# PEER expert gathers: up and down row of a pick in one transfer, down rows multiplied on four 64x64 quarters of TensorE

## The reference, cut to what matters

```
s1, s2 = scores of the token's query against keys[0], keys[1]      # (128, 8, 128) each
v1, i1 = top_k(s1, 16); v2, i2 = top_k(s2, 16)
sv, pos = top_k(all 256 sums v1 + v2, 16);  eidx = i1 * 128 + i2 at pos
g   = softmax(sv)
act = gelu(einsum('thkd,td->thk', u_tab[eidx], xb))                 # up rows
out = einsum('thk,thkd->td', g * act, v_tab[eidx])                  # down rows
```

## Time and profile before

| | |
|---|---|
| median of 3 runs | 4980.2 us (4972.65 to 4982.28) |
| the profiled execution, its own time | 4965.21 us |
| span of the profiled execution, first to last instruction | 4963.3 us |
| mean granted TensorE clock | 0.850 of full speed |
| busy: PE, PEld, DVE, ACT, POOL | 3325.2, 1520.2, 2724.8, 734.2, 2441.9 us |
| moved by DMA | 1566.78 MB |
| first gather issued, last `add_up` starts | 923.6 us, 4943.9 us |

### The profile page before, as it was taken

The page is one execution under the profiler, slowest core; times in us unless marked ns, Lnnn a source line. Parts: engine busy times, 40 slices in busy tenths (PEclk is TensorE's granted clock), DMA queues, the critical chain, the costliest instruction groups (busy, mean ns, idle before and its releaser), DMA issues. The chain is left out here.

```text
span 4963.3 us, 57041 instructions
## 1 busy us (share of the span) xinstructions
PE 3325.2 (67%) x21891; PEld 1520.2 (31%) x21891; DVE 2724.8 (55%) x6844; ACT 734.2 (15%) x1873; POOL 2441.9 (49%) x2579
## 2 busy tenths in 40 slices
PE   8897888782655676745676666566667656555677
PEld 4443775540011331322232244134313411210111
DVE  1357443497665575555666565555566556556410
ACT  1045231110000031000021023103202200000000
POOL 0000000156666566556666655655566566566665
PEclk9995998896888888977887888788888888788899
DMA  5160001599999999999999998998999899999998
GB/s 206 54 271 22 6 5 44 185 355 362 371 372 384 393 371 368 398 379 381 385 388 368 379 389 331 367 390 318 346 384 399 323 358 406 362 371 374 371 367 324
DMA packets 426081, 1566.78 MB, mean 316 GB/s; under 512 B 50278, under 2 KB 51393, under 8 KB 419281
## 3 DMA queue, kind: packets, MB, share of 16 engines
q0 software_dynamic: 369088, 1342.53, 70.3%
q1 hardware_dynamic: 56424, 220.51, 11.6%
q10 hardware_dynamic: 298, 0.09, 0.0%
HBM read 1559.84 MB, written 3.10 MB: 315 GB/s over the span
## 5 line engine op out<-in xcount | busy, mean ns | idle before, releaser
L2212 PE MATMUL t_ps<-t_vring,t_wz 128*32 128x512 f32 x4864 | 1641.0, 721 | 868.7 <-DMA t_vring<-in_peer_v,t_eidT 467.0
L1691 DVE SCALAR_TENSOR_TENSOR t_uring<-t_uring,t_ps 128x1024 f32<-128x1024 f32 x1280 | 1555.6, 1217 | 1039.2 <-DMA t_uring<-in_peer_u,t_eidx 779.2
L1567 POOL DMA_INDIRECT t_vring<-in_peer_v,t_eidT x1216 | 1152.5, 948 | 921.1 <-PE t_ps L2212 383.0
L1553 POOL DMA_INDIRECT t_uring<-in_peer_u,t_eidx x1280 | 1220.1, 953 | 654.2 <-issue 327.7
L2212 PEld LDWEIGHTS t_ps<-t_vring,t_wz 128*32 128x32 f32 x4864 | 293.0, 122 | 1907.6 <-issue 980.2
L1544 POOL MEMSET t_wz<- 128x2064 f32 x1 | 1.8, 1817 | 876.9 <-POOLq L132 876.9
L2115 PE MATMUL t_ps<-t_early 128*128 128x128 f32 x1550 | 257.6, 324 | 205.7 <-remote 128.6
L2115 PEld LDWEIGHTS t_ps<-t_early 128*128 128x128 f32 x1550 | 226.2, 228 | 289.5 <-issue 261.1
L1922 ACT ACTIVATE t_early<-ident,vec 128x128 f32<-128x128 f32 x775 | 263.1, 394 | 310.8 <-PE t_ps L2115 167.0
L2097 PE MATMUL t_ps<-t_hT,t_wg 128*128 128x128 f32 x1280 | 180.5, 298 | 56.3 <-DMA t_wg<-in_cv_w_pw 37.7
L2097 PEld LDWEIGHTS t_ps<-t_hT,t_wg 128*128 128x128 f32 x1280 | 164.1, 207 | 131.4 <-issue 103.4
(11 more groups left out here) (365 smaller groups left out, 3679.2 us busy)
## 6 DMA issues: line engine op xcount, KB each, us to landing
t_wq<-in_peer_w_q SPq DMA_DIRECT2D x112, 512.0 KB
ev_mod_ring<-in_mod_w SPq DMA_DIRECT2D x48, 1024.0 KB, 9.2
t_wg<-in_cv_w_pw SPq DMA_DIRECT2D x80, 512.0 KB
t_uring<-in_peer_u,t_eidx POOLq DMA_INDIRECT x1280
t_wq<-in_cv_w_pw SPq DMA_DIRECT2D x40, 512.0 KB
t_vring<-in_peer_v,t_eidT POOLq DMA_INDIRECT x1216
t_pair<-modrows SPq DMA_DIRECT2D x25, 512.0 KB
ev_wring<-in_ab_w_in SPq DMA_DIRECT2D x21, 512.0 KB, 3.5
```

What stands on the lines that cost most here:

```text
L1553: pool.indirect_dma_start(uring[:, n % RU, :], None, u_tab, bass.IndirectOffsetOnAxis(ap=eidx[:, s % 2, r:r + 1], axis=0)).then_inc(u_in[n ...
L1567: pool.indirect_dma_start(vring[:, n % RV, :], None, v_tab, index).then_inc(v_in[n % RV], 16)
L1691: V.scalar_tensor_tensor(uring[:, n % RU, :], uring[:, n % RU, :], 1.0, hp, ALU.mult, ALU.mult, accum_out=dots[:, j % 2, r:r + 1]).then_in ...
L2212: last = nc.tensor.matmul(acc[32 * g:32 * g + 32, a * 512:(a + 1) * 512], wz[:, first:first + 32], ring[:, n % size, a * 512:(a + 1) * 512 ...
```

## The change

The two tables are laid side by side in HBM, `peer_uv` with rows of 2048 floats (8 KB). One indirect DMA for each pick brings up and down row of 128 tokens into one ring `ring` of R = 8 buffers of 8 KB a partition (in slot 0 only six of them: the last two still hold `hT0`). DVE's dot reads the first half and now takes the activations from SBUF (`h_of(j)`). As the down rows now stand with a token on each partition, the product with the weights is one with a diagonal matrix: for every two picks ACT takes the gelu of two dots, multiplies each with its gate, and makes two 128x64 tiles `dg` (two 64x64 diagonals one above the other). PE multiplies them in 64x64 quarters: the even pick on the quarters low to low and high to high into `straight`, the odd pick on low to high and high to low into `crossed`. At the end of a slot ACT copies `crossed` to SBUF and four matmuls with `eye` add its halves, exchanged, to `straight`. A ring buffer is free when PE has used it. Slots are now 10. The softmax gates are taken head by head, and the latents' query and score products become a side of slot 0 (`score_tick`, from tick 0 to 84).

```diff
-    RU, RV = 6, 8
+    R = 8
+    HALF = P // 2
+    DIAGS = 6
+    place = [n % (R - 2) if n < PICKS else (R - 2 + n - PICKS) % R for n in range(JOBS * PICKS)]
+    freed_by = [max([m + 1 for m in range(max(0, n - 2 * R), n) if place[m] == place[n]], default=0) for n in range(JOBS * PICKS)]
+    score_tick = lambda b: max(0, 6 * (b - 2))
...
             def _(pool):
-                nc.gpsimd.memset(wz[:], 0.0).then_inc(S["cleared"], 1)
-                for s in range(JOBS + 1):
+                for s in range(JOBS):
                     for r in range(PICKS):
...
+                        n = s * PICKS + r
+                        if r % G == 0:
+                            pool.wait_ge(S["chosen"], s * PH + r // G + 1)
+                        if freed_by[n]:
+                            pool.wait_ge(S["used"], freed_by[n])
+                        elif place[n] >= R - 2:
+                            pool.wait_ge(S["q_done"], Q0)
+                        pool.indirect_dma_start(ring[:, place[n], :], None, table,
+                                                bass.IndirectOffsetOnAxis(ap=eidx[:, s % 2, r:r + 1], axis=0)).then_inc(row_in[place[n]], 16)
...
                 def dot(j, r):
-                    dve.wait_ge(u_in[n % RU], 16 * (n // RU + 1))
-                    V.scalar_tensor_tensor(uring[:, n % RU, :], uring[:, n % RU, :], 1.0, hp, ALU.mult, ALU.mult,
+                    dve.wait_ge(row_in[place[n]], 16 * fills[n])
+                    V.scalar_tensor_tensor(ring[:, place[n], 0:D], ring[:, place[n], 0:D], 1.0, h_of(j), ALU.mult, ALU.mult,
                                            accum_out=dots[:, j % 2, r:r + 1]).then_inc(S["u_used"], 1)
...
+                def weigh(j, c):
+                    m, r = j * PICKS // 2 + c, 2 * c
+                    act.wait_ge(S["u_used"], 2 * m + 2)
+                    if m:
+                        act.wait_ge(S["diag_set"], 2 * m)
+                    nc.scalar.activation(wgt[:, r:r + 2], dots[:, j % 2, r:r + 2], ACT.Gelu).then_inc(S["gelu_done"], 1)
...
+                    for b in range(2):
+                        nc.scalar.activation(wgt[:, r + b:r + b + 1], wgt[:, r + b:r + b + 1], ACT.Copy, scale=gate[:, j % 2, r + b:r + b + 1]).then_inc(S["wgt_done"], 1)
+                    for b in range(2):
...
+                        nc.scalar.activation(dg[:, n % DIAGS, :], eye[:], ACT.Copy, scale=wgt[:, r + b:r + b + 1]).then_inc(S["diag_set"], 1)
+
+                def take_crossed(j):
+                    act.wait_ge(S["used"], (j + 1) * PICKS)
...
+                    nc.scalar.copy(y, crossed).then_inc(S["crossed_out"], 1)
...
+                    for c in range(PICKS // 2):
+                        run_sides(sides, 2 * c)
+                        n = s * PICKS + 2 * c
+                        one, two = place[n], place[n + 1]
+                        if c == 0 and s:
+                            pe.wait_ge(S["gated"], s)
+                            pe.wait_ge(S["crossed_out"], s)
+                        pe.wait_ge(row_in[one], 16 * fills[n])
+                        pe.wait_ge(row_in[two], 16 * fills[n + 1])
+                        pe.wait_ge(S["diag_set"], n + 2)
+                        for a in range(2):
+                            cols, rows = slice(a * 512, (a + 1) * 512), slice(D + a * 512, D + (a + 1) * 512)
+                            ends = dict(start=(c == 0), stop=False)
+                            nc.tensor.matmul(straight[low, cols], dg[low, n % DIAGS, :], ring[low, one, rows], **ends)
+                            first = nc.tensor.matmul(straight[high, cols], dg[high, n % DIAGS, :], ring[high, one, rows], **ends)
+                            ends = dict(start=(c == 0), stop=(c == PICKS // 2 - 1))
+                            nc.tensor.matmul(crossed[high, cols], dg[low, (n + 1) % DIAGS, :], ring[low, two, rows], **ends)
+                            second = nc.tensor.matmul(crossed[low, cols], dg[high, (n + 1) % DIAGS, :], ring[high, two, rows], **ends)
+                        first.then_inc(S["used"], 1)
+                        second.then_inc(S["used"], 1)
                     run_sides(sides, PICKS)
+                    pe.wait_ge(S["crossed_out"], s + 1)
+                    for a in range(2):
+                        cols = slice(a * 512, (a + 1) * 512)
+                        nc.tensor.matmul(straight[low, cols], eye[high, :], y[high, cols], start=False, stop=True)
+                        last = nc.tensor.matmul(straight[high, cols], eye[low, :], y[low, cols], start=False, stop=True)
+                    last.then_inc(S["joined"], 1)
```

302 lines of the change are left out of this document (105 added, 197 removed).

## The result

The changed kernel takes 4683.9 us (median of 4 runs, 4680.3 to 4694.3), the kernel before 4976.4 beside it (4968.0 to 4982.3): ratio 0.942, 95% interval 0.940 to 0.944. That is 5.8% faster. The profiled run took 4694.3 us, of which the span is 4692.5.

A forecast was written before the change was run, and what follows sets the result against it. DMA transfers were taken to bound the kernel: 923.6 before the first gather + 3381 gathers + 354 other loads + 235 idle + 18.7 after = 4912 us of span, 4929 for the median, range 4800 to 5085.

The forecast's parts named there:

- the idle time: DMA idle after the first gather: 55 us at start and slot 0, 165 in slots 1 to 9, 15 at the end.
- rival D: POOL no longer near its limit, so DMA stalls shrink to 130 us in all: 4824 us; chance 0.16.
- The frame: Whole kernel: DMA transfers set the time; engine work counts only through 181 us of rest or a gathered byte's price.
- PE's pair: Two picks on PE: 16 matmuls on four quarters running at once, 1.91 us a pair.
- rival C: PE quarters sharing a PSUM bank take turns: 3.8 us a pair, 5079 us in all; chance 0.04.
- ACT's load: Added ACT work beside the picks: 1.7 us a pair with waits, some 290 table loads, 2200 us in all, no bound.
- the end of a slot: After a slot's last row lands, 11.1 us until a buffer frees, covered by 16 to 21 us of transfers: no cost.
- the price of a gather: Queue q0: 2.641 us for each of 1280 gathers, 3381 us, 105 saved, bounds 0 and 286.
- the faster refill: POOL refills a drained queue at 1.24 us per 2.64 us of transfer, taking away some idle time in slots 1 to 9.
- a new risk in the shared ring: Buffers held from issue until PE uses the down half; eight buffers give 21.1 us, absorbing jitter up to 8 us.
- rival A: Ring too short at ticks 58 to 110 of five conv slots, ticks of 3.75 us: 5079 us; chance 0.22.
- Start and slot 0: Idle DMA before the first pair, expected at 988 us, and in slot 0, bursts some 2 us each: 55 us.

The follow-up runs named there:

- e13: Changed kernel plus extra gathers ahead of the first pick, 96 of 8 KB rows, then 96 times two of 4 KB, waiting only for landings: 5144.4 us.
- e7: Changed kernel with six places of the ring in use throughout, not eight from slot 1 on: 4903.7 us.
- e10: Changed kernel with nine small memsets on GpSimd ahead of each gather: 4825.1 us.
- e1: Changed kernel with each pick's up and down rows fetched by two gathers of 4 KB rows from two tables: 5106.1 us, 1.0145 of the kernel before.
- e2: Changed kernel with six small memsets on GpSimd ahead of each gather: 4689.7 us.
- e6: Changed kernel with eight small memsets on GpSimd ahead of each gather: 4699.2 us.
- e9: Changed kernel with seven places of the ring from slot 1 on: 4698.6 us.
- e8: Changed kernel with slot 0's query bursts begun at tick 2 + 6b and each cut into two halves at neighbouring pairs: 4632.4 us.
- e11: e8 with the last ten of seventeen context bursts moved beside pairs 0 to 9 of slot 0, and latents' bursts from tick 20 on: 4609.5 us.
- e18: e3 with e1's two 4 KB gathers a pick and the dots' second operand copied to PSUM once a slot: 5167.4 us, 1.024 of the kernel before.
- e3: Changed kernel without quarters: one 128x128 diagonal a pick, four in store instead of six, one accumulator, no join: 4752.1 us.

## Why the prediction was wrong

By its own sum: 4912 us of span forecast, 4692.5 measured, 220 less. The first gather came 4.5 later and the work behind is 0.7 longer; q0 is 108 less, q1 6 less, the idle time 111 less. Either of the two large misses alone would have left the time inside the range. The range was also narrower than the prediction's own bounds: it went down to rival D alone, and with its lower bounds for both terms (2.50 us a gather, 80 us for slots 1 to 9) the sum is 4663.

- **The frame was right**: transfers set the time, engine work does not. PE's pair at 1.9 us (1.9 measured), no turns between row tiles in one bank (rival C would have given 3.8), ACT's load without consequence (262 table loads of 1.283 us beside the picks where some 290 were forecast; its work for a pair 1.27 us where 1.5 was), the end of a slot at no cost but for slot 0, where the queue of six places runs empty for some 5 us at 1405. The rule of the Trainium skill (TensorEngine Tiling (Array Packing), Gotcha 1: PSUM Pressure) behind rival C does not bind for these quarters, which write different partitions of the bank. The loads have 0.02 us of idle time before them and, where the next input is ready, 0.01 behind, so the 2.66 us with a drain of the Trainium skill (ScalarE: Activation LUTs, What ACT_TABLE_LOAD costs) are not paid here; that the drain comes before the load, as the prediction puts it, the page doesn't say. From the start of its dot to the end of its pair a pick takes 6.9 us; the prediction had 7.8 and 5.1 from the landing for the two picks.
- **The step that failed first is the price of a gather**, "I take 2.641, since the gathers too run with gaps": 2.557 by share, 108 us too much. Its row was a stretch of loads with gaps; the one without a gap beside it said 2.50, and slots without sides now run at 2.50. A packet's price is not a constant that comes with its size: e13 has 4 KB and 8 KB rows within 3% of each other when the queue is full (2.56 and 2.49 us), and e7 and e10 have 8 KB packets 4% dearer when it isn't. The 2.724 of before was a price with a queue that ran thin at times. Price and idle time were summed as two terms of their own; in e7 and e1 both grow, in e10 nearly the price alone.
- **The step that failed most is the idle time**: "Slots 1 to 9 ... I take 165". With the end it was put at 180 us and is 36. The prediction set the faster refill against a new risk in the shared ring and took them as equal. Rival D (0.16) had the size of the idle time, 130 us, but not the reason: with the rows left at 8 KB and GpSimd slowed to 2.35, 2.65 and 2.85 us a gather the rest stays at 108, 109 and 136 us (e2, e6, e10). The first of these is 92% of the queue's 2.557, as 1.24 was 91% of 1.362 before. The time rises by 6 to 11, 15 to 20 and 141 to 146 us, and it is q0 that grows. The idle time comes back with six places (210) and with two gathers a pick (241). The risk in the ring was put in the wrong place: rival A expected it where all engines work, and there, in ticks 58 to 110 of the five conv slots, a tick takes 2.5 to 2.9 us (A: over 3.4). The ring is indeed near its end, but everywhere: eight places turn over in 20.1 us at the queue's pace and 17.0 to 17.5 are needed (e7, e9), so some 3 us are to spare and not the 8 that the prediction gave; at seven the cost is 0.4%, at six 4.8%.
- **Start and slot 0** were taken as 55 and are 88: the first pair came at 1002 us and not at 988, and a burst of 7 us costs a ring of six places more than the "2 us each". Moving and cutting the bursts (e8, e11) takes 70 us off the time.
- **That the change moves the dots' operand to SBUF was priced on VectorE alone** (0 to 87 us hidden; 1224 ns a dot measured for 1217). What it does to GpSimd (issue 1.14 us in the mean for 0.95) was not seen; it is a fifth of the 1.04 us a gather that e2 adds at a cost of 6 to 11 us.

What stays open: why e1 loses 422 to 427 us, and with it how the merged gather took the idle time out of slots 1 to 9. Of the 412 us by which e1's stretch is longer 281 are q0, 14 q1 and 117 the rest. A row of 4 KB by itself makes some 90 of them (e13); the operand's place is not it (e18); GpSimd's own time, first to last gather without its waits for PE, is 2.83 us a pick in e1 and (3872 - 227)/1280 = 2.85 in e10, which loses 141 to 146. The difference shows up as waits for places (514 us in e1, 227 in e10), and q0 has 153 us more in e1. In e10 the memsets stand ahead of the wait and pass while GpSimd would wait anyway, in e1 both gathers stand behind it; that this makes the 280 us of difference is argued from the two programs and not tested. So it is shown that one gather of 8 KB rows is what gives the gain (e1), and that a full queue makes each packet cheaper (e7, e10); how the rest of the gain comes about is not.

## What to carry to other kernels

When a kernel is bound by gathers, count what one issue of GpSimd brings. Where the issues take as long as the queue needs for their bytes the packets themselves get dearer (e10), and rows twice as long can pay far more (here 276 us) than their price in a full queue says (some 90). Measure the stay in a ring by shortening it by a place or two: the time is flat until it breaks (7 places +0.4%, 6 places +4.8%). Once transfers bind, look for what stands ahead of the first freed place and for single waits longer than the ring's slack; two such moves in the order of work gave 2%.

## What the runs showed of the hardware

- Packets of an indirect gather of 8 KB rows go whole: median 312 ns, 163,840 of them for 1280 gathers; 4 KB: 159 to 162. With a queue that runs thin the median stays and the mean grows: 318 to 331 ns (e10, e7).
- TensorE's granted clock in slot 9 is 0.75 in the changed kernel, with PE busy 58% of the window, and 0.99 in e3, the same picks with 128x128 diagonals, with PE busy 74%: nearly all at the upper level of 2.4 GHz. The DMA share is 1.00 and 1.01 in the two, so the lower clock cost nothing there.
- An indirect gather takes GpSimd 0.94 us to issue, whether its rows are 4 or 8 KB (0.937 and 0.942 in e13), and up to 1.36 beside dots of VectorE with both operands in SBUF.
